# Zeros through TensorE ahead of the loads, and a later request for the second input tile, in a float32 forward pass of two transformer blocks

## The reference

```python
for l in range(DEPTH):                       # DEPTH = 2
    h = rms_norm(x, mix_norm_g[l])           # x * rsqrt(mean(x*x) + eps) * gain
    proj = h @ w_in[l]                       # q, k, v of two attentions, gate logits
    ...                                      # stick-breaking attention, sliding-window attention
    x = x + merged @ w_out[l]
    h2 = rms_norm(x, mlp_norm_g[l])
    x = x + jnp.square(jax.nn.relu(h2 @ w_up[l])) @ w_down[l]
```

## Time and profile before

| | |
|---|---|
| median of 3 runs | 2220.04 us (2218.41 to 2225.88) |
| the profiled execution | 2222.17 us, its span 2220.4 us |
| TensorE's busy time, DVE's, ACT's, POOL's | 2192.9, 1552.9, 1101.5, 213.4 us |
| mean granted TensorE clock | 0.999 |
| bytes read from HBM | 392.90 MB, 177 GB/s over the span |

### The profile page before, as it was taken

The page is one execution under the profiler, slowest core; times in us unless marked ns, Lnnn a source line. Parts: engine busy times, 40 slices in busy tenths (PEclk is TensorE's granted clock), DMA queues, the critical chain, the costliest instruction groups (busy, mean ns, idle before and its releaser), DMA issues.

```text
span 2220.4 us, 33556 instructions
## 1 busy us (share of the span) xinstructions
PE 2192.9 (99%) x13406; PEld 1889.2 (85%) x13406; DVE 1552.9 (70%) x2159; ACT 1101.5 (50%) x1659; POOL 213.4 (10%) x207
## 2 busy tenths in 40 slices
PE   8999999999999999999999999999999999999998
PEld 7888888888888888888789988888888887998887
DVE  5777845677864775776887687567657788777774
ACT  4745434555543544445454554455444555355443
POOL 0000200001210210010004001011101000310110
PEclk9999999999999999999999999999999999999999
DMA  6445565434555755554435565566556544465554
GB/s 239 143 137 182 186 203 185 154 133 171 189 190 180 252 187 191 185 183 154 159 117 171 171 209 190 191 227 202 191 172 201 170 145 143 131 202 181 189 190 133
DMA packets 108666, 395.58 MB, mean 178 GB/s; under 512 B 12320, under 2 KB 12464, under 8 KB 108256
## 3 DMA queue, kind: packets, MB, share of 16 engines
q1 hardware_dynamic: 103680, 374.91, 50.7%
q0 software_dynamic: 4832, 18.53, 2.6%
HBM read 392.90 MB, written 1.05 MB: 177 GB/s over the span
## 4 chain that ended last, share of the span: by engine, by line
PE 92%; DVE 5%; ACT 2%; issue 1%; DMA 1%; DVEq 0%; ACTq 0%; POOLq 0%
PE psum L448 44%; PE psum L599 27%; PE psum L598 14%; DVE w_low L405 2%; PE psum L817 2%; PE psum L962 2%; PE psum L939 1%; PE psum L926 1%; ACT w_high L402 1%; PE psum L1335 0%; PE psum L897 0%; DMA pages<-in_gains 0%; ACT attn_p L1119 0%; PE psum L1349 0%; DVE xs L2411 0%
## 5 line engine op out<-in xcount | busy, mean ns | idle before, releaser
L405 DVE TENSOR_TENSOR w_low<-ring,w_high 128x1024 fp32r<-128x1024 f32 x704 | 861.9, 1236 | 318.7 <-ACT w_high L402 317.9
L402 ACT ACTIVATE w_high<-ring 128x1024 fp32r<-128x1024 f32 x704 | 733.8, 1055 | 509.0 <-DMA ring<-in_weights 505.5
L599 PE MATMUL psum<-xT,w_high 128*128 128x512 f32 x2784 | 980.8, 396 | 0.0
L598 PE MATMUL psum<-xT,w_low 128*128 128x256 f32 x2784 | 790.4, 284 | 5.0 <-DVE w_low L405 5.0
L599 PEld LDWEIGHTS psum<-xT,w_high 128*128 128x128 f32 x2784 | 523.0, 188 | 120.5 <-issue 1.0
L598 PEld LDWEIGHTS psum<-xT,w_low 128*128 128x128 f32 x2784 | 526.6, 189 | 8.8 <-issue 6.2
L448 PE MATMUL psum<-w_high,hidden 128*128 128x512 f32 x1216 | 376.6, 390 | 0.0
L448 PEld LDWEIGHTS psum<-w_high,hidden 128*128 128x128 f32 x1216 | 228.2, 188 | 47.1
L448 PE MATMUL psum<-w_low,hidden 128*128 128x512 f32 x608 | 236.6, 389 | 0.0
L448 PE MATMUL psum<-w_high,xT 128*128 128x512 f32 (+2 forms) x640 | 193.2, 382 | 0.7 <-DVE xT L776 0.6
L448 PE MATMUL psum<-rounded_pages,w_high 128*128 128x256 f32 x896 | 165.6, 286 | 0.0
(11 more groups left out here) (241 smaller groups left out, 2073.8 us busy)
## 6 DMA issues: line engine op xcount, KB each, us to landing
ring<-in_weights SPq DMA_DIRECT2D x702, 512.0 KB, 3.5
pages<-in_affine POOLq DMA_DIRECT2D x16, 512.0 KB, 6.0
ring<-in_weights SPq DMA_DIRECT2D x8, 440.0 KB, 3.2
pages<-in_gains POOLq DMA_DIRECT2D x4, 512.0 KB, 5.2
pages<-in_mem POOLq DMA_DIRECT2D x2, 1024.0 KB, 6.6
pages<-in_bias POOLq DMA_DIRECT2D x2, 988.0 KB, 10.7
ring<-in_weights SPq DMA_DIRECT2D x4, 384.0 KB, 2.9
pages<-in_rows POOLq DMA_DIRECT2D x2, 512.0 KB, 5.9
```

The lines of the kernel that those rows point to most:

```text
L402: eng.activation(high, raw, ACT.Copy).then_inc(self.flag("w_rounded").sem, 1)
L405: eng.tensor_tensor(self.w_low[:, piece % SLOTS, 0:width], raw, high.bitcast(F32), ALU.subtract).then_inc(self.flag("w_split").sem, 1)
L598: pe.matmul(out[:, 0:SEQ], low, self.xT_high[:, k, :], start=(k == 0), stop=False, skip_group_check=True)
L599: m = pe.matmul(out, high, self.xT[:, k, :, :].rearrange("p x s -> p (x s)"), start=False, stop=(k == kn - 1), skip_group_check=True)
```

## The change

Three edits. POOL waits for p0 between the request for the gain and the request for the second input tile. DVE sets one quarter of the later `xT` buffer's first slice to zero (128 partitions by 512 floats) as its first instruction. TensorE waits for that and multiplies the zeros sixteen times (128 stationary columns, 512 moving columns), into the bank that the first product later overwrites, before it waits for the identity matrix.

```diff
@@ opening, gpsimd
         pool.dma_start(c.page(16), io["gains_1"][0:1, :].to_broadcast([P, D])).then_inc(c.flag("gain_in").sem, 16)
+        c.wait_landed(pool, 0)
         pool.dma_start(c.x[:, 1, :], io["x_in"][:, 1, :]).then_inc(c.flag("x_in1").sem, 16)
         c.wait_landed(pool, 1)
@@ opening, vector
+        dve.memset(c.xT[:, 0, :, :].bitcast(F32), 0.0).then_inc(c.flag("warm_set").sem, 1)
         dve.memset(c.idle[:, :], 0.0).then_inc(c.flag("idle_set").sem, 1)
@@ block_1, tensor
+        zeros = c.xT[:, 0, :, :].rearrange("p x s -> p (x s)")
+        pe.wait_ge(c.flag("warm_set").sem, 1)
+        for _ in range(16):
+            pe.matmul(c.psum[:, 0, :], zeros[:, 0:P], zeros, start=True, stop=True)
         pe.wait_ge(c.flag("ident_in").sem, 16)
```

## The result

| | before | after |
|---|---|---|
| median of 8 runs each | 2221.30 us (2217.59 to 2225.88) | 2227.97 us (2221.95 to 2231.86) |
| ratio after / before | | 1.0023, 95% interval 1.0013 to 1.0032 |
| span of the profiled execution | 2220.4 us | 2225.2 us |

The change makes the kernel slower by 0.23%, 5.1 us (2.9 to 7.1); a repeat later gave 1.0018 (1.0009 to 1.0028). The two medians of the table differ by 6.7 us, 0.30%, near the upper end of that interval. That is within 0.3%, as forecast, and on the forecast's side, but the loss is larger than the +3.0 us predicted, which lies at the lower end of the interval, and the median lies 0.5 us over the top of my range (2227.5).

What follows compares the result with a forecast made beforehand. TensorE was taken to bound the kernel, with only the opening touched. Late x_in1 gives T - 13.75 = +2.25 us, the low clock 0.75: +3.0 on the median 2220.04 makes 2223.0 us, range 2218.5 to 2227.5.

Steps and rivals of the forecast that it cites:

- What bounds, and that the opening's shift carries on: TensorE, busy 99% of the span, bounds; a microsecond won or lost before about 20.4 us stays to the end.
- The memset 0.4: Opening, DVE: zeroing 128x512 takes 0.4 us, covered by DVE's wait for the gain until 9.2 us.
- zeros over by 8.2: Opening, TensorE: sixteen zero matmuls from about 1.4 us end between 5.0 and 8.2, before the transposes at 10.36.
- The zeros stand in the way: Opening: weight loads don't overlap matmuls, zeros end at 13.6; alone +2.6 us, nothing more with late x_in1; chance 0.05.
- The clock falls by the first products: Opening, TensorE: the zeros' high clock is gone by 12.8 us, 0.6 likely, changing nothing in the forecast time.
- x_in1's landing: Opening: x_in1, requested at 9.4 instead of 2.0 us, takes 6.6 us and lands at 16.0, ends 14.6 and 17.3.
- T: When DVE starts the second xT low half: 13.03 us before, 16.0 forecast; later work shifts by T - 13.75.
- The gain, kept at 9.1: Opening: the gain's transfer lands at 9.1 us, against 9.17 before, within bounds of 6.6 and 9.2.
- One of my signs of being wrong: Opening: the forecast counts as wrong if the gain's transfer lands well before 9 us.
- The first rival ("in time"): Opening: p0 lands early, x_in1 by 13.7 us; T = 12.6, shift -1.15, 2218.9 us; chance 0.15.
- the clock behind the wait: Opening, TensorE: after idling, low clock may add 1.4 us to the matmuls of k = 2 to 5; 0.75 taken.
- The rival with T = 19.6: Opening: x_in1 again takes 10.2 us and the clock is low; +7.25 us, 2227.3 us; chance 0.08.

Runs made afterwards that it cites:

- fourteen fillers: Changed kernel plus fourteen extra matmuls on TensorE ahead of k = 2 of the first product; ratio to the kernel before 1.0004.
- DVE's wait moved: Changed kernel with DVE's wait for x_in1 placed behind tile 0's second low half and the splits of p1 to p3; ratio to before 1.0001.
- eight fillers: Changed kernel plus eight extra matmuls on TensorE ahead of k = 2 of the first product; ratio to the kernel before 1.0014.
- by SP: Kernel before with SP requesting x_in1: behind p0, 1.0007; with more zeros 0.9989, repeated 0.9998; behind p2, DVE's wait also moved, more zeros, 0.9995.
- again: The changed kernel unaltered, profiled and timed a second time beside the kernel before; ratio 1.0018.
- wait alone: Kernel before plus only POOL's wait for p0 ahead of x_in1, without the zeros; ratio to before 1.0024.
- the wait for p1: Changed kernel with POOL waiting for p1 instead of p0 ahead of x_in1; ratio to the kernel before 1.0020.

## Why the prediction was right, and where it was off

- **What bounds, and that the opening's shift carries on: right.** Of the six timings with tile 1 less G 4 us or more over before, five came out 3.1 to 5.3 us slower (ratio less 1, times 2221), and one, with fourteen fillers, 0.9 us (from -1.3 to +3.1). The seven others lie between -2.4 and +1.6 us. Within each group the medians don't follow the size. For the fourteen fillers the profile shows a reason: of its 4.8 us at tile 1 only 2.0 were left at the instruction near 1002 us (1004.18), with TensorE at its quicker pace in between (last section). Whether the other executions had that pace is not recorded.
- **The memset 0.4, measured 0.48; zeros over by 8.2, measured 7.0; no cost: right.** (The memset covers the whole first slice of xT, 512 floats in each partition, not a quarter of it.) "The zeros stand in the way" fell: they take 0.34 us each in the mean.
- **The clock falls by the first products: right**, in five of the seven profiles with sixteen zeros. In the other two (DVE's wait moved, eight fillers) the gain came before 8 us, TensorE's gap ahead of the transposes was 1.5 and 1.7 us against 2.5 to 3.8, and it held to the first products. Transposes did run fast: 1.23 us for eight instead of 1.94. In these two the high clock was still there behind them, where I had expected the zeros' effect to be gone.
- **x_in1's landing: right, by two errors.** I put T at 16.0 and it was 16.06, from an issue at 9.4 (8.83) and 6.6 us to landing (7.2; 7.0 to 7.9 over all runs with the wait). Of my bounds the 7.9 was the nearer, not the 5.2 of calmer stretches.
- **The gain, kept at 9.1: the landing was 8.3, and no effect of the wait shows.** One of my signs of being wrong, the gain well before 9, came in this profile; it says nothing about the wait. G with x_in1 asked for at 2.0 us was 9.26, 8.88 and 7.84; with POOL's wait 8.43, 9.44, 7.45, 9.90, 8.29, 7.82 and 9.72; by SP 7.90, 8.30, 9.17 and 7.54. The means are 8.7, 8.7 and 8.2. The argument from POOL's queue stands; what moves the landing by 2 us from run to run is not settled. The first rival ("in time") needed it, and fell.
- **The term that was mis-sized: the clock behind the wait.** I took half of 1.4 us, put at 0.75 (half is 0.7), on a coin's chance. It came in every profile where TensorE was left idle for 2.8 us or more just ahead of k = 2: tile 1 at T + 8.0 to T + 8.2 in changed, again and eight fillers, and T + 9.3 and T + 9.0 in wait alone and p1, in place of T + 6.65. That is 1.3 to 2.7 us instead of 0.75. With 1.5 the sum would have been T - 12.25 = +3.8 at tile 1, as measured (24.22 - 20.40); 24.22 lies 0.2 us past the 22.6 to 24.0 that I had named. The rest, 5.1 against 3.8, is within the interval.
- **The rival with T = 19.6** fell: the 10.2 us held the wait behind the gain in the same queue, and alone x_in1 took 7.0 to 7.9.

## What to carry to other kernels

Before a transfer is put off to give another one room, look at what stands behind the instruction that waits for it, on each engine: here a wait in the middle of DVE's queue held the split of p1, which POOL saw landed at 10.15 us, until 16.7. Moving that wait behind the independent work took 1.8 of the opening's 4.5 us away, without touching the transfer, and no loss was left that the timing could show. Keeping TensorE busy can pay only if nothing else sets the start of its real work, and only if it is not left idle too long before that work begins: here the clock fell behind 2.5 us and held behind 1.7. No version here was shown to be faster by it.

## What the runs showed of the hardware

**TensorE's high clock outlasts a gap or not.** After the same sixteen zeros (busy to about 7 us) it was 0.50 from 12 us on in the changed kernel and 1.00 until 18.5 in the one with DVE's wait moved, where the transposes came a microsecond earlier (8.54 us). The same 2.48 us idle stretch at 1100 us, present in both kernels, was followed by 1.00 in before and by 0.50 in after. First the window behind it in before, then the wait's row in after, then the window behind that one:

```profile
1101.00:1103.00 2.00, 2.00 (x14) 1.65 (x13) 2.00 (x2) 0.00 (x0) 0.00 (x0) 1.00 0.00 0
```
```profile
1102.73 0.36 PE L598 MATMUL psum<-xT,w_low 128*128 128x256 f32 x1 [2.48 <-DVE w_low L405]
```
```profile
1104.00:1107.00 3.00, 3.00 (x12) 2.31 (x11) 3.00 (x3) 0.00 (x0) 0.00 (x0) 0.50 0.00 0
```

It is 14 matmuls in 2 us against 12 in 3, so 1.3 of these 3 us are lost. One such low stretch costs about 1.5 us: an instruction of ACT behind it (line 1119 in both) starts at 1115.91 in before and 1120.32 in after, +4.4 where it was +2.9 ahead of it. Over the profiles the clock fell at this place in eleven of fourteen; what decides was not tried. It is part of the spread of 8 to 10 us between the first eight runs of each kernel.

**TensorE has two paces at full clock.** The 512-column matmuls of one feed-forward stretch (line 599, granted clock 1.00) take 399 ns in one profile and 391 in another. First before, then the kernel with DVE's wait moved, both 760 to 800 us (busy us, mean ns):

```profile
L599 PE MATMUL psum<-xT,w_high 128*128 128x512 f32 x115 | 40.7, 399 | 0.0
```
```profile
L599 PE MATMUL psum<-xT,w_high 128*128 128x512 f32 x116 | 40.3, 391 | 0.0
```

Ten of the fourteen profiles have 399 there and four 391: wait alone, DVE's wait moved and both fillers. In the changed kernel, its repeat and the wait for p1, all at 399, the shift at the instruction near 1002 us is within 0.3 us of that at tile 1. In the four at 391 it is 2.4 to 3.0 us less, with nothing changed there. Elsewhere two profiles of one and the same kernel differ, first changed, then changed again, both 1320 to 1360 us:

```profile
L599 PE MATMUL psum<-xT,w_high 128*128 128x512 f32 x116 | 40.3, 391 | 0.0
```
```profile
L599 PE MATMUL psum<-xT,w_high 128*128 128x512 f32 x114 | 40.3, 399 | 0.0
```

So the pace can change from execution to execution; whether it does in the stretch at 760 us, or goes with the build there, is open, as no kernel with two profiles shows both. The cause was not looked for. Worth up to 3 us here, it is larger than what the opening could give, and one reason why effects of 1 us do not show in medians of a dozen runs.
